# Raw rows behind three norms, scaled at eviction, a paired third and fourth tile, and shared probability copies in a two-block transformer kernel

## What is computed

```python
def rms_norm(x, gain):
    y = x * lax.rsqrt(jnp.mean(x * x, axis=-1, keepdims=True) + 1e-6)
    return y * gain

def first_block(x, ...):
    for l in range(2):
        proj = rms_norm(h, norm_mix[l]) @ w_in[l]
        (hq, hf, hi, hg, nq, kc, vc, ksl, vsl, ksw, vsw, ngate) = jnp.split(proj, ...)
        o_hg = hgrn2_mixer(hq, hf, hi, hg, lb[l], hg_gnorm[l])   # f = lb+(1-lb)*sigmoid(hf), k = 1-f
        o_nsa = nsa_mixer(nq, kc, vc, ksl, vsl, ksw, vsw, ngate, ...)  # compressed, selected, windowed attention
        h = h + jnp.concatenate([o_hg, o_nsa], axis=-1) @ w_out[l]
        gu = rms_norm(h, norm_ffn[l]) @ w_ffn_in[l]
        h = h + (jax.nn.silu(gu[..., :D_FF]) * gu[..., D_FF:]) @ w_ffn_out[l]

def second_block(x, mem, ...):
    h = rms_norm(x, g_mix)
    fq, fk, fv, f_logit, dq, dk, dv, gate_a, gate_b = jnp.split(h @ w_in, offsets, axis=-1)
    merged = sigmoid(gate_a) * (fox_attention(...) @ w_branch_a) + sigmoid(gate_b) * (diff_attention(...) @ w_branch_b)
    x = x + merged @ w_out
    x = x + cross_attention(rms_norm(x, g_cross), rms_norm(mem, g_mem), w_cq, w_ckv, w_co)
    x = x + hier_moe(rms_norm(x, g_ffn), ...)     # 32 experts, two for each token
    return rms_norm(x, g_final)
```

## Time and profile before

| what | number |
|---|---|
| median of the runs | 2558.77 us (2553.39 to 2562.32, 3 runs) |
| the profiled execution | 2559.99 us; its span 2558.2 us |
| mean granted TensorE clock of it | 0.977 |
| TensorE matmuls busy | 2399.5 us, 94% |
| GpSimd, VectorE, ScalarE busy | 1110.9, 1073.4 and 664.1 us |
| costliest groups of TensorE | L2062, L2061, L2063 on xl, xh: 537.0, 520.9, 511.0 us |
| chain that ended last | TensorE 76%, DMA 14%, VectorE 6% |
| a ring tile, from issue to landing | 3.5 us; a half of an expert's matrix 25 to 30 us |

### The profile page before, as it was taken

One profiled execution on the slowest core, in us unless ns is written; L12 is line 12 of the kernel. 1 busy time (PEld: TensorE's weight loads), 2 busy tenths in 40 slices (PEclk: granted clock), 3 DMA queues, 4 the chain that ended last, 5 costly groups with the idle time before them and its releaser, 6 DMA issues.

```text
span 2558.2 us, 36724 instructions
## 1 busy us (share of the span) xinstructions
PE 2399.5 (94%) x12852; PEld 1731.5 (68%) x12852; DVE 1073.4 (42%) x1985; ACT 664.1 (26%) x1298; POOL 1110.9 (43%) x766
## 2 busy tenths in 40 slices
PE   7999999999999999999999999999998899888885
PEld 5878778888878787678888878776685533333332
DVE  4565764122344756762213363444466511111113
ACT  5424552111015325641110022034504200000001
POOL 4861116666767931136667756543163011111111
PEclk9998999999999998999999999999999899999997
DMA  4222002333222221013323322221135399999996
GB/s 143 75 66 91 26 18 92 97 98 98 91 91 75 75 84 58 18 50 98 92 97 99 122 77 84 82 76 57 50 99 214 143 392 406 407 405 401 410 411 265
DMA packets 78173, 373.29 MB, mean 146 GB/s; under 512 B 11232, under 2 KB 11360, under 8 KB 53344
## 3 DMA queue, kind: packets, MB, share of 16 engines
q1 hardware_dynamic: 71904, 360.09, 39.1%
q0 software_dynamic: 5280, 8.40, 1.0%
q10 hardware_dynamic: 864, 3.15, 0.3%
HBM read 367.92 MB, written 12.58 MB: 149 GB/s over the span
## 4 chain that ended last, share of the span: by engine, by line
PE 76%; DMA 14%; DVE 6%; issue 2%; ACT 1%; SPq 0%; DVEq 0%; POOLq 0%; POOL 0%; ACTq 0%
PE PS L2061 18%; PE PS L2063 18%; PE PS L2062 18%; DMA arena<-w_up 13%; PE PS L2729 4%; PE PS L2442 2%; PE PS L2471 2%; PE PS L2183 1%; PE PS L2756 1%; PE PS L2136 1%; PE PS L2456 1%; PE PS L2419 1%; PE PS L2119 1%; DVE xl L1207 1%; PE PS L2534 1%
## 5 line engine op out<-in xcount | busy, mean ns | idle before, releaser
L607 POOL TENSOR_SCALAR whi<-ring 128x1024 fp32r<-128x1024 f32 x256 | 286.5, 1119 | 905.2 <-PE PS L2063 693.6
L610 POOL TENSOR_TENSOR wlo<-ring,whi 128x1024 fp32r<-128x1024 f32 x256 | 649.6, 2538 | 21.3
L2062 PE MATMUL PS<-xl,whi 128*128 128x512 f32 x1376 | 537.0, 390 | 0.0
L2061 PE MATMUL PS<-xh,whi 128*128 128x512 f32 x1312 | 520.9, 397 | 0.2
L2063 PE MATMUL PS<-xh,wlo 128*128 128x512 f32 x1312 | 511.0, 389 | 0.0
L2729 PE MATMUL PS<-arena,xraw 128*64 128x512 f32 x512 | 255.8, 650 | 65.4 <-DMA arena<-w_up 58.5
L2062 PEld LDWEIGHTS PS<-xl,whi 128*128 128x128 f32 x1376 | 259.1, 188 | 53.1 <-issue 3.4
L2061 PEld LDWEIGHTS PS<-xh,whi 128*128 128x128 f32 x1312 | 246.3, 188 | 56.5 <-issue 5.6
L2063 PEld LDWEIGHTS PS<-xh,wlo 128*128 128x128 f32 x1312 | 246.2, 188 | 52.1
L2730 PE MATMUL PS<-arena,xraw 128*64 128x512 f32 x512 | 256.9, 653 | 0.0
L2729 PEld LDWEIGHTS PS<-arena,xraw 128*64 128x64 f32 x512 | 71.3, 148 | 213.3 <-issue 206.0
(11 more groups left out here) (501 smaller groups left out, 4043.2 us busy)
## 6 DMA issues: line engine op xcount, KB each, us to landing
ring<-ring_w SPq DMA_DIRECT2D x280, 512.0 KB, 3.5
arena<-w_gate SPq DMA_DIRECT2D x64, 1024.0 KB, 25.0
arena<-w_up SPq DMA_DIRECT2D x64, 1024.0 KB, 27.7
xraw<-w_down SPq DMA_DIRECT2D x32, 1024.0 KB, 29.1
arena<-w_down SPq DMA_DIRECT2D x30, 1024.0 KB, 29.6
arena<-y_dram SPq DMA_DIRECT2D x8, 512.0 KB, 6.6
xT<-xT_in SPq DMA_DIRECT2D x2, 1024.0 KB, 6.8
out<-arena SPq DMA_DIRECT2D x4, 512.0 KB, 2.6
```

The lines of the kernel that those rows point to most:

```text
L607: nc.gpsimd.tensor_scalar(hi, ring[:, t % RING, :], 1.0, 0.0, ALU.mult, ALU.add).then_inc(sems["whi"], 1)
L610: nc.gpsimd.tensor_tensor(wlo[:, t % RING, :], ring[:, t % RING, :], hi, ALU.subtract).then_inc(sems["split"], 1)
L2061: mm(out, a[0], b[0], start=start, stop=False, skip_group_check=skip_group_check)
L2062: mm(out, a[0], b[1], start=False, stop=False, skip_group_check=skip_group_check)
```

## The change

- **Raw rows.** Ahead of the first-block norms and the first norm of block two, ScalarE writes `rh`, the rounded product of row and gain without rstd, chunk by chunk beside the squares, and VectorE the rest, `rl` (`raw_lows`). `behind_norm` on TensorE runs the high parts of tile 0 on `rh`, the mean of squares (into bank 4), the high parts of tile 1, and the low parts of both. VectorE multiplies the two finished tiles by rstd as it copies them out of PSUM (`raw_tile`); ScalarE's sigmoid of tiles 0 and 1 follows in place.
- **First pair.** Tiles 2 and 3 run as a pair on normed rows (`first_pair`): high parts of both, then low parts of both.
- **Cross norm.** The two query tiles of the cross attention run on unnormed rows alone, and VectorE scales them at the eviction. The normed rows are not made there.
- **Padding.** `keep_warm` ahead of these norms' tiles and of the mean goes; at the start of the program eight stand.
- **Splits.** Three more spare places for rounded weights take the last two tiles of a layer and the third of the next, so that GpSimd splits the next layer's tiles 0 and 1 ahead of the pair's end (`back=4`). Block two's output and cross tiles are handled alike.
- **Start.** SP loads the first half of the rows, tile 0, the matrices, the second half, then tiles 1 to 3.
- **Experts.** Gate and up halves share one semaphore, `wGU`.
- **Turned tiles.** ScalarE copies every fourth (L1088 of the changed kernel), VectorE the others; `turned` waits for either.
- **Tables.** Steps are in another order, and the last but one piece of decay products moves from tile 18 to 19.

```diff
@@ GpSimd
-            def split(base, t, second=None):
+            def split(base, t, second=None, back=2):
...
-                if second is None:
-                    pool.wait_ge(sems["tile"], base + (t - 1 + RING))
+                if second is None and back:
+                    pool.wait_ge(sems["tile"], base + (t + 1 - back + RING))
...
-                    split(base, t, whi_last if t == T_LAYER - 1 else None)
...
+                    split(base, t, spare[t - (T_LAYER - 2)] if t >= T_LAYER - 2 else None)
+                split(base, T_LAYER, back=4)
+                split(base, T_LAYER + 1, back=4)
+                pool.wait_ge(sems["xs"], l * FFC + FFC)
+                split(base, T_LAYER + 2, spare[2])
@@ ScalarE
+            def raw_norm(l):
...
+                for c in range(KO):
+                    act_e.wait_ge(sems["h"], nth("h", l, c + 1 - 8))
+                    nc.scalar.activation(rh[:, c, :], xT[:, c, :], ACT.Identity, scale=lcol[:, C_MIX + c:C_MIX + c + 1]
+                                         ).then_inc(sems["rh"], 1)
+                    nc.scalar.activation(sqe[:, c, :], xT[:, c, :], ACT.Square).then_inc(sems["sq"], 1)
+                mean_rstd(l, 0, 4)
...
+                    if it and it["k"] % 4 == 3:
...
+                        nc.scalar.activation(PT4[3][:, 0:n], PS[:, 4, 0:n], ACT.Identity).then_inc(sems["pta"], 1)
@@ VectorE
                 elif kind == "norm":
-                    v.wait_ge(sems["params"], nth("params", l, 1))
                     v.wait_ge(sems["rstd"], nth("rstd", l, i + 1))
+                    raw_tile(l, 0, kT[:, 0, :])
+                    raw_tile(l, 1, kT[:, 1, :])
...
+                elif kind == "feat" and i >= 34:
+                    v.wait_ge(sems["rstd"], nth("rstd", l, 3))
+                    v.wait_ge(sems["tile"], nth("tile", l, tile2_of(i) + 1))
+                    nc.vector.scalar_tensor_tensor(out=cqT[:, i - 34, :], in0=PS[:, i % 2, :], scalar=0.125, in1=rstd,
+                                                   op0=ALU.mult, op1=ALU.mult).then_inc(sems["evac"], 1)
...
-                    if it:
+                    if it and it["k"] % 4 < 3:
@@ TensorE
+            def behind_norm(l, t, n, j, high, low):
+
+                high_parts(l, PS[:, 0, :], t, *high)
+                mean_square(l, n, j, bank=4)
+                high_parts(l, PS[:, 1, :], t + 1, *high)
+                low_part(l, PS[:, 0, :], t, *low)
+                low_part(l, PS[:, 1, :], t + 1, *low)
...
-                    if i in (0, 7):
+                    if i == 7:
                         keep_warm(6, 3)
...
-                        mean_square(l, i, i, done=nth("h", l, 1))
...
+                    behind_norm(l, B_CQ, 2, 2, (xh, "xh", 8), (xl, "xn", 16))
...
-                    pe.wait_ge(MS["wG"][2 * (u % 2) + h], (i + u // 2) * 16 + 16)
-                    pe.wait_ge(MS["wU"][2 * (u % 2) + h], (i + u // 2) * 16 + 16)
+                    pe.wait_ge(MS["wGU"][2 * (u % 2) + h], (i + u // 2) * 32 + 32)
```

```diff
-    "gram4 gram5 rs0 feat13 gram6 gram7 rs1 feat14 feat15 feat16 gram8 rr0 rs2 gram9 feat17 gram10 rs3 gram11 rr1 "
-    "feat18 gram12 rr2 rs4 gram13 feat19 gram14 gram15 gatem0 hi0 hi1 hi2 rr3 hi3 rr4 rs5 v0 v1 ket0 cmpt0 rr5 ket1 "
-    "cmpt1 ket2 cmpt2 state0 state1 cmpt3 gatet0 state2 state3 cmpt4 hn0 hn1 cmpt5 hn2 cmpt6 cmpt7 hn3 cmpo0 "
+    "rs0 feat13 rr0 gram6 rs1 feat14 gram7 rr1 feat15 rs2 feat16 gram8 feat17 gram9 rs3 gram10 feat18 gram11 rs4 "
+    "gram12 rr2 gram13 rs5 gram14 feat19 gram15 gatem0 rr3 hi0 hi1 hi2 hi3 rr4 gatet0 v0 v1 ket0 rr5 ket1 ket2 "
+    "cmpt0 cmpt1 state0 state1 cmpt2 state2 cmpt3 state3 cmpt4 hn0 hn1 cmpt5 hn2 cmpt6 cmpt7 hn3 cmpo0 attention0 "
```

More of the change, by code:

```diff
@@ L2068, in keep_warm, with weights, high_parts @@
                     mm(PS[:, bank, 0:MEM], ones_d, mats[:, 0:MEM], start=True, stop=True)
[L2070 to L2073 removed]
+            def weights(t, cols, hi=None):
+                return (whi[:, t % 2, :] if hi is None else hi)[:, cols], wlo[:, t % RING, cols]
+            def high_parts(l, out, t, x, done, first):
+                pe.wait_ge(sems["split"], nth("split", l, t + 1))
+                for c in range(KO):
+                    pe.wait_ge(sems[done], nth(done, l, first + c + 1))
+                    for j, w in enumerate(weights(t, slice(c * P, c * P + P))):
+                        mm(out, w, x[:, c, :], start=(c == j == 0), stop=False, skip_group_check=True)
@@ new lines, in low_part @@
+            def low_part(l, out, t, x, done, first):
+                for c in range(KO):
+                    pe.wait_ge(sems[done], nth(done, l, first + c + 1))
+                    ins = mm(out, whi[:, t % 2, c * P:c * P + P], x[:, c, :], start=False, stop=(c == 7),
+                             skip_group_check=True)
+                ins.then_inc(sems["tile"], 1)
+            def behind_norm(l, t, n, j, high, low):
[4 more added lines that the diff above has]
+                low_part(l, PS[:, 1, :], t + 1, *low)
@@ L2459, in pv_pair @@
             def pv_pair(l, one, two):
-                pe.wait_ge(sems["pt"], nth("pt", l, two["k"] + 1))
+                turned(l, one["k"])
+                turned(l, two["k"])
                 qt, first = one["qt"], one["k"] % NSA_QT == 0
@@ L2827 @@
 PARAMS2_AT = 204
[L2828 removed]
+DECAYED_AT = [7, 9, 11, 13, 15, 17, 19, 19]
 A_CH = 2 + ROPES + 4
```

219 lines of the change are left out of this document (150 added, 69 removed), and 18 rows, old and new, of tables (ACT_STEPS, DVE_STEPS, PE_STEPS).

## The result

The change makes the kernel slower: 2588.85 us median (2586.47 to 2592.16, 4 runs) against 2557.09 us for the kernel before, ratio 1.0122 with a 95% interval of 1.0103 to 1.0141. The forecast was 2530 us. The profiled execution took 2592.16 us, its span is 2589.9 us, 31.7 more than before.

A forecast was written before the change was run, and what follows sets the result against it. TensorE was taken to set the pace ahead of the experts, weight streaming inside them. Norms 25.1, copies 4, state steps 2.6, less 2 for chains, sum to 29.7 us off the profiled 2559.99: forecast 2530 us, range 2515 to 2546.

The forecast's parts named there:

- What bounds the kernel: Whole kernel: TensorE sets the pace ahead of the experts, weight streaming inside them; a gain ahead moves the end equally.
- Copies of turned tiles: Attention: 36 of 144 copies move from VectorE to ScalarE, cutting TensorE's waits; 4 us gained.
- the opposite: Rival, attention: ScalarE's copy waits for a turn and delays the next exponential; 43 us lost, 2578 us, chance 0.02.
- The start of attention: Fourth head's norm on ScalarE, table load and query low part on VectorE ahead of the first maximum; zero, -4 to +6.
- The norms: Layer two and block two: raw rows replace padding and waiting, fifth tile at 29.7 not 34.5 us; 4.8 us gained each.
- The start: Program start: first norm with raw rows and new load order, 42.7 us against 48.1; 5.4 us gained.
- The cross norm: Cross attention's norm: both query tiles run on unnormed rows, 14.1 us against 24.2; 10.1 us gained.
- State steps: Ahead of the last state step, a compression step fills TensorE's wait; 2.6 us gained in two layers.
- Chains behind the norm: Scans, decays and GpSimd's products start later against TensorE; 2 us lost, bounds 0 and -10.
- Clock: Rival, norms: the clock falls in the new gap without padding; 13 us lost in sum, 2543 us, chance 0.10.
- the signs of being wrong: Norms gaining under 3 us, gram waits over 3 us a layer, clock 0.50 behind a norm, growing exponential waits in attention.

The follow-up runs named there:

- the three edits: The changed kernel with ScalarE's copy ahead of the exponential, the third split early (fifth behind the eighth row), and query low parts moved earlier: 2542.92 us, ratio 0.9949.

## Why the prediction was wrong, point by point

**What bounds the kernel** was right: from the experts on, nothing changed (527.0 and 527.1 us), and what was lost ahead of them moved the end by as much.

**Copies of turned tiles: the step that failed.** I priced them at 4 us gained, and gave the opposite a chance of 0.02. They cost 19.5 us in both layers against VectorE copying all, 0.54 us for each of 36. The failing sentence is that ScalarE has slack, read from a busy share: 15.4 of 20 us. The share says that the work fits, not that the copy is done in time. TensorE has only the next scores and the next turn between a turn and the product that needs it; ahead of ScalarE's copy stand an exponential that itself waits for a maximum, and a scaling. I wrote the mechanism down among the rivals but put the delay on the exponential, while the trace and the run with the copy ahead show it on the product. Moved ahead, the copy gains 6.7 us, more than my 4. The copies didn't turn the sign alone: 29.7 less 23.5 would still be 6 us faster. (By my own terms the sign turns at 25.7 / 36 = 0.7 us a copy, not at 0.9.) The norms with raw rows and the start of attention had to lose as well.

**The start of attention** I set at zero, "-4 to +6", and named the right pieces. It was +2.5 us of wait in each layer, and clock behind it: with the query low parts moved, 1.9 us of wait and 5 us of time a layer came back. I had blamed the norm on ScalarE as much as the low part. Putting the norm back alone gave nothing, while VectorE's order gave 1.9 of the 2.5 us; whether ScalarE's order holds the rest, no run tells.

**The norms.** Each step had its size but for those where VectorE works beside a split, and for the last raw row, which is also late since ScalarE's product with the gain holds up the squares: it came at 4.9 us, not 2.9. The pair started at 18.3, not 15.4; its rows took 8.2 us, not 5.1; the fifth tile's wait was 2.5 us in block two and the forecast 2.0 in the others. I had the third tile's split beside the unnormed low parts, where TensorE's matmuls cover it, and wrote that the exclusion changes nothing. I overlooked the fourth tile's: it waits for the second tile's end, which is the moment at which VectorE starts on the normed rows. With that one moved the norm is 31.4 us, within 1.7 of my 29.7.

**The start** was 7 us off, by the timelines for the same reason: splits beside VectorE's sums, low parts and rows. ScalarE's sixteen operations ended at 16.9, near my 16.4, but VectorE's last sum of squares only at 19.5.

**The cross norm** was right, 8.9 us for 10.1. No split runs beside its rows. Its gain reached the end: the distance to the kernel before falls from 38.6 us at the last add ahead of the cross norm to 31.7 us at the last add behind the cross attention, and stays there.

**State steps** were right: the wait is gone in both layers, and the stretch from the last gram to attention is 1.9 us shorter in layer one and 4.1 in layer two. **Chains behind the norm**, named at 2 us in all: the stretch of the grams is 1.7 us longer in each layer (86.9 and 85.2 us). **Clock**: it fell at the norms, as a rival had it, but padding gave back at most 0.7 us a norm, within the spread of that stretch; and its mean over attention went from 0.97 to 0.94, which no part of the forecast had. Of the signs of being wrong, three were seen: norms that gain nothing, the clock of 0.50 behind a norm, and a longer wait for an exponential, at attention's start alone.

From 29.7 us less, as forecast, to 31.7 us more, as the spans show, it is 61.4 us: 23.5 are the copies (19.5 and the 4 not gained), 10 the start of attention, 3.2 the rest of attention, 20.4 the three norms with raw rows, 1.2 the cross norm, 5.2 the stretches not looked at, 0.1 the experts, less 2.2 that the states and grams gained beyond the forecast. The parts of attention come from edits run one at a time, one execution each, and the three edits together gained 7 us less than alone, so they are a reckoning and not a measurement.

## What to carry to other kernels

Work moved to a less busy engine is late by what stands ahead of it in that engine's queue; compare that delay with the time between producer and consumer on the engine that waits, and place the moved work ahead of what has slack. Before moving VectorE's passes with two SBUF inputs, list GpSimd's subtractions that will fall on them: here each cost its whole length, 2.67 us, and the pass that waits may be the critical one. A table of steps should be read per engine down to the first instruction of the next stage.

## What the runs showed that I had not expected

- GpSimd's one-input rounding pass is held as well: with the fifth split behind the rows it took 5.79 us, where it takes 1.05, while VectorE subtracts low parts with two inputs from SBUF.

```profile
1550.16 5.79 POOL L617 TENSOR_SCALAR whi<-ring 128x1024 fp32r<-128x1024 f32 x1 [12.54 <-DVE xraw L1512]
```

- With the state steps' wait of 1.3 us back, the stretch from the last gram to attention was 13.3 us longer in one layer and 3.6 us in the other of one execution (93.1 and 83.4 us against 79.8). What the clock takes behind such a wait differs from time to time, and in one layer of the change (83.6 us) it fell without one.
- An earlier first product (11.85 in place of 14.89 us) moved the fifth tile by 0.5 us only.
